# Scoring half of a cross attention inside the query projection, and starting the output projection head by head

## The chip, the cores and the metric

The kernel runs on one core of one Trainium2 chip. The metric is the device time of one execution in microseconds (us), the median of several runs. Engines: PE (TensorE, matmuls and transposes, with PEld its weight loads), ACT (ScalarE), DVE (VectorE), POOL (GpSimd), and SP, which here only issues transfers. Each engine runs its own list of instructions in order; they meet at semaphores alone.

## What is computed

A chain of two transformer layers of one kind and one of another, for 256 tokens of width 1024, in float32. Each of the first two layers is: a gated feed-forward (FFN), a mixer (a pooling one in layer 0, a sparse attention, "NSA", in layer 1), a cross attention to 256 memory tokens, and a second FFN. The change touches the cross attention and the NSA mixer.

```python
def memory_cross_attention(h, mem_n, w_q, w_kv, w_o):
    B, S, D = h.shape                      # 1, 256, 1024
    Hx, dh = XATTN_HEADS, XATTN_HEAD_DIM   # 4, 256
    q = (h @ w_q).astype(F32).reshape(B, S, Hx, dh) * dh ** -0.5
    ...
    p = jax.nn.softmax(jnp.einsum('bqhd,bkhd->bhqk', q, k), axis=-1)
    o = jnp.einsum('bhqk,bkhd->bqhd', p, v).reshape(B, S, D)
    return o.astype(h.dtype) @ w_o
```

The NSA mixer projects `h` to queries, keys, values and gates, compresses blocks of keys and values with a small two-layer network, attends to the compressed blocks, to selected blocks and to a window for each of 16 heads, mixes the three by gates, and multiplies by `nsa_w_o`.

## The kernel before

**Weights and products.** A weight matrix is read in slabs of 128x2048 values into four slots of `raw`. ACT copies a slab rounded into `whi` (`split` in ACT's program, line L759), DVE subtracts to get the rest `wlo` (`split` in DVE's, L1308), and PE makes each product of three matmuls (`parts`, L2007 to L2009): high by low, low by high, high by high. A projection to 1024 columns is two chunks of 512; a chunk uses a pair of slots (0 and 1, or 2 and 3) and one half of PSUM's eight banks, the halves taking turns (`half_of_banks`). `chunks` in ACT's and DVE's programs interleaves: the splits for the next chunk (or, in the last chunk, those of the next stage's first chunk, `next_slabs`), and then the evacuation of the present one.

**Cross attention.** The stage `query` makes the queries, transposed, in two chunks; each chunk holds two of the four heads. `cross` then has 8 units, one for each head and half of the tokens. For a unit PE makes the scores (L2211), DVE their maximum (`top`, L1528), ACT the exponentials with their sum (`exps`, L950), DVE the reciprocal and the scaling (`weigh`, L1534 and L1535), PE two transposes (`turn`, L2221), ACT the copy to SBUF (`keep`, L958). For each head PE then makes probabilities times values (`values`, L2230), ACT and DVE split the result into `aT_hi` (L964) and `aT_lo` (L1540). Three buffers are in rotation, and the scores of a unit are made two units ahead. `project` multiplies by `xattn_w_o`.

**Stages.** A stage begins with `enter` (the engine waits until ACT and DVE have both left the stage before) and ends on ACT and DVE with `leave` (a drain, L743 on ACT and L1291 on DVE). `keep_clock(n)` issues n matmuls on zeros (L2048); nothing reads them.

**NSA.** `nsa_compress` has its own four slabs; after it, ahead of the attention's first instructions, ACT and DVE split the first two slabs of `nsa_w_o`. `nsa_attend` has 32 units with a similar chain (L2321 scores, L1644 maximum, L1030 exponentials, L1653 and L1656 scaling, L2332 transposes, L2349 values), and PE issues 20 matmuls on zeros behind its first scores.

## Time and profile before

| | |
|---|---|
| median of 3 runs | 1831.32 us (1831.2 to 1831.63) |
| the profiled execution | 1832.79 us, of which the span of the profile is 1830.7 us |
| granted clock, mean | 0.954 of full |
| PE busy | 1685.5 us (92%) |
| DVE busy | 1037.7 us (57%) |
| ACT busy | 790.0 us (43%) |
| layer 0: second query chunk / cross / projection begins | 307.6 / 320.2 / 347.4 us |
| layer 1: second query chunk / cross / projection begins | 1039.5 / 1052.1 / 1078.2 us |
| layer 1: NSA attention / its projection begins | 921.65 / 997.00 us |

The profiled execution lasted 2.09 us more than its span, and 1.47 us more than the median. In a row of the timeline the numbers are start and duration in us; a bracket at its end holds how long the engine had been idle and what released it. PE's matmuls are pipelined: a row of n instructions lasts longer than n steps by the tail of the last one. The granted clock is 1.00 at 2.4 GHz and 0.50 at 1.2 GHz.

### The profile page before, as it was taken

Reading aid. Unit: us, or ns where it says so; the run is one execution under the profiler, and the core shown is the slowest. Engines: PE = TensorE matmul, PEld = TensorE weight load, DVE = VectorE, ACT = ScalarE, POOL = GpSimd, SP = SyncE. Lnnn points to the kernel's source line nnn. Section 1 sums busy time; section 2 is a strip of 40 time slices with the busy share of each in tenths; the row PEclk is TensorE's granted clock in tenths of the full one; section 3 lists DMA queues with packets and bytes.
Section 4 is the critical chain, followed back from the end, with each engine's and each line's share of the span. In section 5 each row is a group of like instructions: output and inputs, shape, how many; then the busy total and the mean of one; then the engine's idle time right before and its main releaser. Section 6 shows DMA issues by size and latency. Waiting matters only on the chain.

```text
span 1830.7 us, 22314 instructions
## 1 busy us (share of the span) xinstructions
PE 1685.5 (92%) x8595; PEld 1397.0 (76%) x8595; DVE 1037.7 (57%) x1326; ACT 790.0 (43%) x964; POOL 96.7 (5%) x143
## 2 busy tenths in 40 slices
PE   6999987899999999989988989999899877889996
PEld 6788867688888788879865867888688663668885
DVE  4577654467765576655565445554557643655553
ACT  4443432355444344333466336555354433244441
POOL 1000000010100000010000021000100110100000
PEclk8999989999999999999989999999899785899998
DMA  8687625077775487743510416556455220435550
GB/s 289 204 282 262 224 100 188 3 264 262 258 231 188 165 267 269 236 135 96 174 59 30 165 51 204 193 189 203 159 182 202 78 103 5 169 130 203 183 183 23
DMA packets 210195, 311.74 MB, mean 170 GB/s; under 512 B 16537, under 2 KB 145589, under 8 KB 209872
## 3 DMA queue, kind: packets, MB, share of 16 engines
q1 hardware_dynamic: 204112, 288.90, 47.2%
q0 software_dynamic: 6016, 21.94, 3.5%
q8 instruction: 42, 0.69, 0.2%
q14 instruction: 25, 0.20, 0.0%
HBM read 306.59 MB, written 4.21 MB: 170 GB/s over the span
## 4 chain that ended last, share of the span: by engine, by line
PE 84%; DVE 6%; ACT 3%; issue 3%; DMA 1%; PEld 1%; POOL 1%; DVEq 0%; PEldq 0%; ACTq 0%; SPq 0%; POOLq 0%
PE ps L2007 25%; PE ps L2009 24%; PE ps L2008 24%; DVE wlo L1308 1%; PE ps L2129 1%; PE ps L2048 1%; PE ps L2230 1%; DMA area<-in_gate_b 1%; PE ps L2058 1%; PE ps L2211 1%; PE ps L2349 1%; ACT xn L1030 1%; PE ps L2436 1%; ACT xn L813 0%; DMA raw<-in_xattn_w_kv 0%
## 5 line engine op out<-in xcount | busy, mean ns | idle before, releaser
L1308 DVE TENSOR_TENSOR wlo<-raw,whi 128x2048 fp32r<-128x2048 f32 x255 | 582.0, 2302 | 237.3 <-ACT whi L759 236.4
L759 ACT ACTIVATE whi<-raw 128x2048 fp32r<-128x2048 f32 x255 | 481.2, 1910 | 206.2 <-PE ps L2009 182.7
L2007 PE MATMUL ps<-wlo,aT_hi 128*128 128x512 f32 (+1 forms) x1280 | 499.3, 390 | 22.8 <-DVE aT_lo L1334 9.2
L2009 PE MATMUL ps<-whi,aT_hi 128*128 128x512 f32 (+1 forms) x1280 | 492.6, 385 | 0.0
L2008 PE MATMUL ps<-whi,aT_lo 128*128 128x512 f32 (+1 forms) x1280 | 492.5, 385 | 0.0
L2007 PEld LDWEIGHTS ps<-wlo,aT_hi 128*128 128x128 f32 x1280 | 243.3, 190 | 73.0 <-issue 14.6
L2009 PEld LDWEIGHTS ps<-whi,aT_hi 128*128 128x128 f32 x1280 | 242.9, 190 | 47.8
L2008 PEld LDWEIGHTS ps<-whi,aT_lo 128*128 128x128 f32 x1280 | 243.5, 190 | 44.9
L2007 PE MATMUL ps<-wlo,hT_hi 128*128 128x512 f32 x480 | 188.0, 392 | 5.4 <-DVE hT_lo L1425 3.0
L2009 PE MATMUL ps<-whi,hT_hi 128*128 128x512 f32 x480 | 187.6, 391 | 0.0
L2008 PE MATMUL ps<-whi,hT_lo 128*128 128x512 f32 x480 | 187.3, 390 | 0.0
L2007 PE MATMUL ps<-aT_lo,whi 128*128 128x256 f32 x600 | 173.4, 289 | 14.8 <-DVE wlo L1308 9.1
L2008 PE MATMUL ps<-aT_hi,wlo 128*128 128x256 f32 x600 | 172.7, 288 | 0.0
L2009 PE MATMUL ps<-aT_hi,whi 128*128 128x256 f32 x600 | 172.5, 288 | 0.0
L2007 PEld LDWEIGHTS ps<-aT_lo,whi 128*128 128x128 f32 x600 | 117.9, 196 | 16.5 <-issue 11.9
L2008 PEld LDWEIGHTS ps<-aT_hi,wlo 128*128 128x128 f32 x600 | 117.9, 197 | 0.1
L2009 PEld LDWEIGHTS ps<-aT_hi,whi 128*128 128x128 f32 x600 | 118.0, 197 | 0.0
L2007 PEld LDWEIGHTS ps<-wlo,hT_hi 128*128 128x128 f32 x480 | 90.4, 188 | 25.3 <-issue 4.1
L2009 PEld LDWEIGHTS ps<-whi,hT_hi 128*128 128x128 f32 x480 | 90.5, 189 | 18.9
L2008 PEld LDWEIGHTS ps<-whi,hT_lo 128*128 128x128 f32 x480 | 90.5, 189 | 18.8
L872 ACT ACTIVATE hT_hi<-ps 128x512 fp32r<-128x512 f32 x44 | 26.3, 598 | 154.8 <-PE ps L2129 154.8
L1350 DVE SCALAR_TENSOR_TENSOR gain<-raw,area,gain 128x256 f32<-128x256 f32 x168 | 81.4, 484 | 5.1
(301 smaller groups left out, 1329.1 us busy)
## 6 DMA issues: line engine op xcount, KB each, us to landing
raw<-in_ffn_w_in SPq DMA_DIRECT2D x176, 512.0 KB, 4.9
raw<-in_ffn_w_out SPq DMA_DIRECT2D x88, 512.0 KB, 4.4
raw<-in_w_ff SPq DMA_DIRECT2D x64, 512.0 KB, 4.8
raw<-in_ada_w SPq DMA_DIRECT2D x48, 512.0 KB, 5.6
raw<-in_w_in SPq DMA_DIRECT2D x48, 512.0 KB, 4.6
raw<-in_xattn_w_kv SPq DMA_DIRECT2D x32, 512.0 KB, 6.9
raw<-in_xattn_w_q SPq DMA_DIRECT2D x16, 512.0 KB, 5.1
raw<-in_xattn_w_o SPq DMA_DIRECT2D x16, 512.0 KB, 4.9
```

The lines of the kernel that those rows point to most:

```text
L759: act.activation(to, of, ACT.Copy).then_inc(hi_ready[slot], 1)
L872: act.activation(hT_hi[:, 0:2, :], ps[:, 6, :], ACT.Copy).then_inc(hT_hi_made, 1)
L1030: last = act.activation(Pb[u % 4][:, c:c + n], Pb[u % 4][:, c:c + n], ACT.Exp, scale=-1.0, bias=nmx4[:, b + j:b + j + 1], accum_out=den4[: ...
L1308: dve.tensor_tensor(lo, of, hi, ALU.subtract).then_inc(lo_ready[slot], 1)
L1350: ins = dve.scalar_tensor_tensor(out=acc, in0=w, scalar=condT[:, k:k + 1], in1=acc, op0=ALU.mult, op1=ALU.add)
L2007: pe.matmul(o, lh, rl, start=start, stop=False, skip_group_check=True)
L2008: pe.matmul(o, ll, rh, start=False, stop=False, skip_group_check=True)
L2009: return pe.matmul(o, lh, rh, start=False, stop=stop, skip_group_check=True)
L2048: pe.matmul(ps[:, bank, :], zero[:, 0:P], zero[:, :], start=True, stop=True, skip_group_check=True)
L2058: last = pe.transpose(ps[:, banks[b], P * k:P * k + P], xn[:, t, P * f:P * f + P], ident)
L2129: last = pe.transpose(ps[:, 6, S * k + P * t:S * k + P * t + P], hs[:, t, HI + P * k:HI + P * k + P], ident)
L2211: last = pe.matmul(ps[:, u % 3, 0:S], qT[:, 2 * h + j, t * P:(t + 1) * P], kT[:, 2 * h + j, :], start=j == 0, stop=j == 1)
```

## The change

The four parts:

- **Scores inside the second query chunk.** After the first of the chunk's four outputs PE makes the scores of units 0 to 3 (heads 0 and 1, whose queries the first chunk gave). DVE takes their maxima between its two splits, ACT the exponentials between its two, and DVE scales all four behind its second split, ahead of evacuating the chunk.
- **A new order of the cross attention.** Four buffers instead of three; PE: transposes of units 0 to 3, scores of 4 to 7, values of heads 0 and 1, transposes of 4 to 7, values of heads 2 and 3. The 12 matmuls on zeros are gone. The outputs' low halves are made last on DVE.
- **Projections wait per head.** PE no longer waits for the stage to end ahead of `project` (cross and NSA): it waits for `o_kept` of a head where it first reads it.
- **NSA.** The two splits of `nsa_w_o`'s first chunk move into `nsa_compress`, and 8 matmuls on zeros are left of 20.

```diff
-            def chunks(count, evac, doubled=(), transfers=(), after=None):
+            def chunks(count, evac, doubled=(), transfers=(), after=None, within=None):
                 for c in range(count):
-                    if c + 1 == count:
+                    if c + 1 == count and within:
+                        split(2 * (count % 2))
+                        within[1]()
+                        split(2 * (count % 2) + 1)
+                    elif c + 1 == count:
                         next_slabs(2 * (count % 2))
...
+                    chunks(2, evac, within=(None, lambda: [self.cross_exps(u) for u in range(4)]))
...
-                    exps(0)
-                    exps(1)
-                    for u in range(8):
+                    for u in range(4):
                         keep(u)
-                        if u + 2 < 8:
-                            exps(u + 2)
-                        if u % 2 == 0 and u:
-                            out_hi(u // 2 - 1)
+                    for u in range(4, 8):
+                        self.cross_exps(u)
+                    out_hi(0)
+                    out_hi(1)
+                    for u in range(4, 8):
+                        keep(u)
+                    out_hi(2)
                     out_hi(3)
...
+                        if v == 0:
+                            split(0)
                         done.next(2 * v)
                         act.wait_ge(consumed[2 * v + 1], done.next(2 * v + 1))
                         act.activation(hid_rows[v], ps[0:4 * N_CMP, v, 0:CMP_HID],
                                        ACT.Gelu_apprx_tanh).then_inc(gelu_made, 1)
+                        if v == 0:
+                            split(1)
...
                     leave()
-                    next_slabs()
...
+                    chunks(2, evac, within=(lambda: [self.cross_top(u) for u in range(4)],
+                                            lambda: [self.cross_weigh(u) for u in range(4)]))
...
+                    if between and j == 1:
+                        between()
                     for k in range(KD):
                         s, r = k // 4, k % 4
+                        if ready and ready(j, k):
+                            pe.wait_ge(o_kept, ready(j, k))
...
+                    def scores():
+                        pe.wait_ge(act_evac, chunk_no.n - 1)
+                        pe.wait_ge(dve_evac, chunk_no.n - 1)
+                        for u in range(4):
+                            self.cross_score(u)
+
+                    chunk(2, 512, turned(bank()), between=scores)
...
-                    score(0)
-                    score(1)
-                    keep_clock(12, 5)
-                    for u in range(8):
-                        if u + 2 < 8:
-                            score(u + 2)
+                    for u in range(4):
                         turn(u)
-                        if u % 2 == 0 and u:
-                            values(u // 2 - 1)
+                    pe.wait_ge(act_evac, chunk_no.n)
+                    pe.wait_ge(dve_evac, chunk_no.n)
+                    for u in range(4, 8):
+                        self.cross_score(u)
+                    values(0)
+                    values(1)
+                    for u in range(4, 8):
+                        turn(u)
+                    values(2)
                     values(3)
                     units.next(8)
                     groups.next(4)
+                    self.heads_ready = lambda j, k: groups.n - 3 + k // 2 if k % 2 == 0 else 0
...
-                    keep_clock(20, 4)
+                    keep_clock(8, 4)
...
+                    self.heads_ready = lambda j, k: groups.n - 1 + j if k == 0 else 0
```

**PE, the end of layer 0's query projection and the cross attention.** Before; ahead of the first row stand the second chunk's 96 matmuls, behind the last one those of the projection:

```order
L2211 MATMUL ps<-area 128x256 x4
L2048 MATMUL ps<-zero 128x512 x12
L2211 MATMUL ps<-area 128x256 x2
L2221 MATMUL ps<-cst,xn 128x128 x2
L2211 MATMUL ps<-area 128x256 x2
L2221 MATMUL ps<-cst,xn 128x128 x2
L2211 MATMUL ps<-area 128x256 x2
L2221 MATMUL ps<-cst,xn 128x128 x2
L2230 MATMUL ps<-area 128x256 x4
```

Of the change; L2239 are scores, L2253 transposes, L2262 values, and between the first row and the second stand the 72 matmuls of the chunk's last three outputs:

```order
L2239 MATMUL ps<-area 128x256 x8
...
L2253 MATMUL ps<-cst,xn 128x128 x8
L2239 MATMUL ps<-area 128x256 x8
L2262 MATMUL ps<-area 128x256 x8
L2253 MATMUL ps<-cst,xn 128x128 x8
L2262 MATMUL ps<-area 128x256 x8
```

The scores of four units have moved into the chunk, the zeros are gone, and what was interleaved unit by unit stands in blocks of four.

**DVE at the same place.** Before (L1516 evacuates a query chunk):

```order
L1516 TENSOR_SCALAR area<-ps 128x512 [waits consumed1]
L1308 TENSOR_TENSOR wlo<-raw,whi 128x2048 [waits hi_ready0]
L1308 TENSOR_TENSOR wlo<-raw,whi 128x2048 [waits hi_ready1]
L1516 TENSOR_SCALAR area<-ps 128x512 [waits consumed3]
L1528 TENSOR_REDUCE small<-ps 128x1 [waits scored,stage_act,stage_dve]
L1528 TENSOR_REDUCE small<-ps 128x1 [waits scored]
```

Of the change (L1538 evacuates, L1548 is the maximum, L1323 the split; behind the last row but one stand three more pairs L1554, L1555):

```order
L1538 TENSOR_SCALAR area<-ps 128x512 [waits consumed1]
L1323 TENSOR_TENSOR wlo<-raw,whi 128x2048 [waits hi_ready0]
L1548 TENSOR_REDUCE small<-ps 128x1 [waits scored] x4
L1323 TENSOR_TENSOR wlo<-raw,whi 128x2048 [waits hi_ready1]
L1554 RECIPROCAL small<-small 128x1 [waits exped]
L1555 TENSOR_SCALAR xn<-xn,small 128x256 [waits dve_step]
...
L1538 TENSOR_SCALAR area<-ps 128x512 [waits consumed3]
```

Four maxima and four scalings now stand ahead of the evacuation of the second chunk, and the second split waits for ACT's, which stands behind four exponentials.

**ACT in NSA's compression.** Before (L1013 is the Gelu, L1055 the attention's first instruction), and then of the change (L761, L1027, L1070):

```order
L759 ACTIVATE whi<-raw 128x2048 x2
L1013 ACT_TABLE_LOAD
L1013 ACTIVATE xn<-ps 60x256 x2
L1016 ACTIVATE gain<-ps 128x60
L1018 ACTIVATE gain<-ps 15x256
L759 ACTIVATE whi<-raw 128x2048 x2
L1055 ACT_TABLE_LOAD
```

```order
L761 ACTIVATE whi<-raw 128x2048 x3
L1027 ACT_TABLE_LOAD
L1027 ACTIVATE xn<-ps 60x256
L761 ACTIVATE whi<-raw 128x2048
L1027 ACTIVATE xn<-ps 60x256
L1032 ACTIVATE gain<-ps 128x60
L1034 ACTIVATE gain<-ps 15x256
L1070 ACT_TABLE_LOAD
```

The two splits ahead of the attention stand before and behind the first Gelu.

## Rows read from the trace of the kernel before

**Rows 1.** The page's first part: busy time and instructions of each engine.

```profile
PE 1685.5 (92%) x8595; PEld 1397.0 (76%) x8595; DVE 1037.7 (57%) x1326; ACT 790.0 (43%) x964; POOL 96.7 (5%) x143
```

**Rows 2.** Groups by line, PE, 1051.5 to 1078 us (layer 1's cross).

```profile
L2211 PE MATMUL ps<-area 128*128 128x256 f32 x32 | 8.1, 382 | 0.9 <-DVEq L1291 0.9
L2230 PE MATMUL ps<-area 128*128 128x256 f32 x32 | 7.7, 383 | 0.5 <-ACT area L958 0.5
L2221 PE MATMUL ps<-cst,xn 128*128 128x128 f32 x16 | 3.3, 290 | 4.2 <-DVE xn L1535 4.2
L2048 PE MATMUL ps<-zero 128*128 128x512 f32 x12 | 3.1, 406 | 0.0
```

**Rows 3.** Timeline of PE, layer 0 (first row) and layer 1.

```profile
307.62 0.28 PE L2007 MATMUL ps<-aT_lo,whi 128*128 128x256 f32 x1
...
1039.53 0.28 PE L2007 MATMUL ps<-aT_lo,whi 128*128 128x256 f32 x1
...
1052.13 1.75 PE L2211 MATMUL ps<-area 128*128 128x256 f32 x7 [0.92 <-DVEq L1291]
...
1064.08 1.03 PE L2211 MATMUL ps<-area 128*128 128x256 f32 x4
...
1078.17 0.47 PE L2007 MATMUL ps<-wlo,aT_hi 128*128 128x512 f32 x1 [1.50 <-ACTq L743]
```

**Rows 4.** Timeline of ACT, layer 0 (first row) and layer 1.

```profile
321.98 1.28 ACT L950 ACT_TABLE_LOAD   x1 [2.05 <-DVE small L1528]
...
1040.22 3.71 ACT L759 ACTIVATE whi<-raw 128x2048 fp32r<-128x2048 f32 x2
...
1053.91 0.47 ACT L950 ACTIVATE xn<-ps,small 128x256 f32<-128x256 f32 x1 [2.07 <-DVE small L1528]
...
1057.96 0.38 ACT L958 ACTIVATE area<-ps 128x256 f32<-128x256 f32 x1 [2.80 <-PE ps L2221]
```

**Rows 5.** Timeline of DVE, layer 1's cross.

```profile
1053.37 0.42 DVE L1528 TENSOR_REDUCE small<-ps 128x1 f32<-128x256 f32 x1 [1.43 <-PE ps L2211]
...
1054.51 0.16 DVE L1534 RECIPROCAL small<-small 128x1 f32<-128x1 f32 x1
1054.71 0.35 DVE L1535 TENSOR_SCALAR xn<-xn,small 128x256 f32<-128x256 f32 x1
```

**Rows 6.** Stretches: length, busy time by engine, granted clock, DMA share, GB/s.

```profile
343.70:351.00 7.30, 5.79 (x16) 4.15 (x15) 2.35 (x2) 4.29 (x3) 0.00 (x0) 0.55 0.01 2
927.60:930.90 3.30, 3.30 (x10) 2.61 (x9) 3.20 (x13) 1.65 (x8) 0.00 (x0) 0.55 1.01 382
937.40:944.10 6.70, 5.64 (x26) 3.95 (x28) 5.67 (x30) 4.37 (x15) 0.00 (x0) 0.50 0.01 4
```

**Rows 7.** Timeline of DVE at the first chunk's end of the output projections.

```profile
359.94 1.28 DVE L1576 TENSOR_TENSOR x<-x,ps 128x512 f32<-128x512 f32 x2 [6.10 <-PE ps L2009]
...
1089.35 1.28 DVE L1576 TENSOR_TENSOR x<-x,ps 128x512 f32<-128x512 f32 x2 [4.71 <-PE ps L2009]
1091.45 7.60 DVE L1308 TENSOR_TENSOR wlo<-raw,whi 128x2048 fp32r<-128x2048 f32 x2 [0.81 <-ACT whi L759]
...
1100.23 1.29 DVE L1576 TENSOR_TENSOR x<-x,ps 128x512 f32<-128x512 f32 x2 [1.19 <-PE ps L2009]
```

**Rows 8.** Timeline of POOL, layer 1's output projection.

```profile
1087.63 9.26 POOL L640 TENSOR_TENSOR area<-area 1x1024 f32<-1x1024 f32 x3 [6.61 <-DMA area<-in_ada_b]
```

**Rows 9.** Timeline of PE and DVE at the start of NSA's attention.

```profile
926.31 6.42 PE L2048 MATMUL ps<-zero 128*128 128x512 f32 x20
...
933.73 0.66 PE L2332 MATMUL ps<-cst,xn 128*128 128x128 f32 x4
...
923.67 4.49 DVE L1308 TENSOR_TENSOR wlo<-raw,whi 128x2048 fp32r<-128x2048 f32 x2 [3.77 <-ACT whi L759]
...
934.31 0.42 DVE L1644 CUSTOM_DVE_ANT_0 xn<-ps,cst 128x256 f32<-128x256 f32 x1 [0.89 <-PE ps L2332]
```

**Rows 10.** Timeline of PE where NSA's output projection begins.

```profile
997.00 0.47 PE L2007 MATMUL ps<-wlo,aT_hi 128*128 128x512 f32 x1 [1.04 <-ACTq L743]
```

More of the change, by code:

```diff
@@ L175, in build @@
         nmx4, den4, rec4 = small[:, 26:34], small[:, 34:42], small[:, 42:50]
+        cross_P = [xnf[:, 256 * b:256 * b + 256] for b in range(4)]
+        cross_bank = (2, 3, 6, 7)
         spare = gain[:, 1, :]
@@ L1308, in split, with chunks @@
                 dve.tensor_tensor(lo, of, hi, ALU.subtract).then_inc(lo_ready[slot], 1)
-            def chunks(count, evac, doubled=(), after=None):
+            def chunks(count, evac, doubled=(), after=None, within=None):
                 for c in range(count):
-                    if c + 1 == count:
+                    if c + 1 == count and within:
+                        split(2 * (count % 2))
+                        within[0]()
+                        split(2 * (count % 2) + 1)
+                        within[1]()
+                    elif c + 1 == count:
                         next_slabs(2 * (count % 2))
@@ L1520, in cross @@
                 def cross(self, l):
                     enter()
[L1523 to L1536 removed]
+                    of_values = half_of_banks(chunk_no.n - 1)
@@ L1545, in cross @@
[L1545 to L1551 removed]
+                    for u in range(4, 8):
+                        self.cross_top(u)
+                    for u in range(4, 8):
+                        self.cross_weigh(u)
+                    for h in range(4):
+                        out_lo(h)
@@ L1620, in nsa_compress @@
                                           ALU.subtract).then_inc(aT_made, 1)
-                    split(2)
-                    split(3)
+                    for s in (2, 3, 0, 1):
+                        split(s)
                     for v in range(2):
@@ L2009, in parts, with chunk @@
                 return pe.matmul(o, lh, rh, start=False, stop=stop, skip_group_check=True)
-            def chunk(pair, n, outs):
+            def chunk(pair, n, outs, ready=None, between=None):
                 before = chunk_no.next() - 2
@@ L2199, in query, with cross_score @@
                     enter()
-                    for c in range(2):
-                        chunk(2 * c, 512, turned(bank()))
-                def cross(self, l):
-                    enter()
-                    def score(u):
-                        h, t = u // 2, u % 2
-                        if u >= 3:
-                            pe.wait_ge(exped, units.n + u - 2)
-                        for j in range(2):
-                            last = pe.matmul(ps[:, u % 3, 0:S], qT[:, 2 * h + j, t * P:(t + 1) * P], kT[:, 2 * h + j, :],
-                                             start=j == 0, stop=j == 1)
-                        last.then_inc(scored, 1)
+                    chunk(0, 512, turned(bank()))
+                    def scores():
[4 more added lines that the diff above has]
+                    chunk(2, 512, turned(bank()), between=scores)
+                def cross_score(self, u):
+                    h, t = u // 2, u % 2
+                    if u >= 4:
+                        pe.wait_ge(exped, units.n + u - 3)
+                    for j in range(2):
+                        last = pe.matmul(ps[:, cross_bank[u % 4], 0:S], qT[:, 2 * h + j, t * P:(t + 1) * P], kT[:, 2 * h + j, :],
+                                         start=j == 0, stop=j == 1)
+                    last.then_inc(scored, 1)
+                def cross(self, l):
+                    stages.next()
+                    of_values = half_of_banks(chunk_no.n - 1)
                     def turn(u):
@@ L2220, in turn @@
                         for m in range(2):
-                            last = pe.transpose(ps[:, 3 + u % 2, P * m:P * m + P], Pb[u % 3][:, P * m:P * m + P], ident)
+                            last = pe.transpose(ps[:, 4 - of_values + u % 2, P * m:P * m + P], cross_P[u % 4][:, P * m:P * m + P], ident)
                         last.then_inc(probs_turned, 1)
@@ L2229, in values @@
                             for m in range(2):
-                                last = pe.matmul(ps[:, 6 + h % 2, S * j:S * j + S],
+                                last = pe.matmul(ps[:, of_values + h % 2, S * j:S * j + S],
                                                  vm[:, m, 256 * h + P * j:256 * h + P * j + P], PTc(h)[:, m, :],
@@ L2246, in cross @@
                     groups.next(4)
+                    self.heads_ready = lambda j, k: groups.n - 3 + k // 2 if k % 2 == 0 else 0
                 def project(self, w, gated=False, part=None):
-                    enter()
                     if gated:
+                        enter()
                         turn_rows()
                         pe.wait_ge(aT_made, c_turned.next(4))
+                    else:
+                        stages.next()
                     for c in range(2):
-                        chunk(2 * c, 512, rows(bank()))
+                        chunk(2 * c, 512, rows(bank()), ready=None if gated or c else self.heads_ready)
                     if part == 0:
```

63 lines of the change are left out of this document (26 added, 37 removed).

## The prediction

> **What bounds the kernel now.** I first read the page: PE is busy 92% of the span, DVE 57%, ACT 43% [rows 1]. So time is to be had where PE waits, or works at the low clock, or does work that nobody reads. Next I read the groups by line for layer 1's cross attention [rows 2] with the timeline of its ends [rows 3]. The second query chunk starts at 1039.53 (the 97th matmul of the stage; the chunk's 96 matmuls end, tail included, at 1052.13 - 0.92 = 1051.21, so without the tail of 0.16 they take 11.5 us), and the projection's first matmul stands at 1078.17: 38.64 us from one to the other. PE's necessary work in them, counted start to start: a score is 4 instructions of 0.217 (four last 1.03, less the tail of 0.38, over three [rows 3]), 0.86 us, and there are 8; values are 8 instructions, 1.73 us, four times; a unit's two transposes about 0.25, eight times; the 12 on zeros 12 x 0.215 = 2.6. So 11.5 + 6.9 + 6.9 + 2.0 + 2.6 = 29.9, and 38.6 - 29.9 = 8.7 us are waits (the idle column shows 0.9 + 0.5 + 4.2 [rows 2] and 1.5 ahead of the projection [rows 3]; the rest is the tail of what ran before each wait). Most of it is for DVE's scaling: PE makes two scores and then wants a transpose whose probabilities still go through maximum, exponential and scaling.
>
> Layer 0 has the same shape, but its chunk starts at 307.62 and the first x-update of the projection stands at 359.94 [rows 3, 7], 52.3 us, against 1089.35 - 1039.53 = 49.8 in layer 1. The stretches say why: from 343.7 to 351.0 the granted clock averages 0.55 with PE busy 5.79 of 7.30 us [rows 6]. In NSA the chain of work starts late, since DVE's two splits run until 928.2 before the first maximum [rows 9], and its projection waits 1.04 us for ACT's drain [rows 10].
>
> **The change, part by part.** Times from the start of the second query chunk, layer 1; a hand-over between engines costs about 0.05 us (maximum 53.37 + 0.42, exponential 53.91, less 0.12 [rows 4, 5]), a drain some 0.2.
>
> *Inside the chunk.* PE: first output 0 to 2.9, four scores to 6.3, three outputs to 15.0 (11.5 + 4 x 0.86). ACT: evacuation, then its first split 0.7 to 2.6 (3.71 for two [rows 4]). DVE: its first split 2.7 to 4.9 (4.49 for two [rows 9]), then the maxima at 4.9, 5.2, 5.7 and 6.5 (0.34 apart, later ones wait for the score). ACT: exponentials of 0.46 each at 5.4, 5.8, 6.3 and 7.0, second split to 9.4. DVE: second split to 11.7, four scalings at 0.45 (reciprocal 0.19, scaling 0.26 to the next start [rows 5]) to 13.5. PE's chunk ends at 15.0, so the evacuation isn't held up: 1.5 us to spare. In layer 0 a table load of 1.28 us stands before the first exponential [rows 4] and leaves 0.2. So three units' worth of waits are paid under 8.6 us of matmuls.
>
> *After the chunk.* Transposes 0 and 1 run at once. The third needs the first copy by ACT, which stands behind evacuation and both drains: copies from 16.05, third transpose at 16.5, a wait of 1.0. Scores 4 to 7 and values of heads 0 and 1 run from 17.0 to 23.9 without a wait, while DVE and ACT do the second four units. The seventh transpose waits 0.6, since the copies of units 4 and 5 (0.28 each; 0.38 long [rows 4]) stand on ACT behind the second output's copy. Values of heads 2 and 3 end at 29.05. The projection reads head 0 first and heads 2 and 3 after 2.7 and 4.1 us, when their low halves have been made (about 28.9 and 30.7). So 27.3 us of work + 1.7 of waits = 29.0. Layer 1 gains 38.6 - 29.0 = **9.6**: 2.6 of zeros and 7.0 of waits. Layer 0: 52.3 - (29.0 + 1089.35 - 1078.17 = 11.2) = **12.1**, if the low stretch goes. I take that, because the waits left to PE come to 1.7 us where they were 8.7, and layer 1 kept its clock with the old ones.
>
> *Given back in layer 1.* POOL starts its loads and three additions for the modulation when DVE leaves the cross. That was 0.05 us after PE began the projection and is now about 1.7 us after (two passes over 128x512 for the last output's halves, and a drain). The additions last 9.26 us [rows 8], and DVE's two splits beside them took 7.60 us where two take 4.49 elsewhere [rows 7, 9]. If they take turns, DVE has 4.5 us of its own and 1.7 us more of POOL's ahead of it: it ends at 1099.05 + 1.7, 20.9 + 1.7 = 22.6 us after the projection's start instead of 20.9, and the x-update which begins at 22.05 [rows 7] is held by 0.6 to 0.85 with the start. I take **-0.8**. Bounds: 0 (they share) and 1.7. The Trainium skill, page "SBUF — State Buffer", says that a VectorE instruction with two SBUF inputs and GpSimd's reads lock each other out for a whole instruction. By that rule the sum has the 0.8; with shared bandwidth it would have 0. The 7.60 against 4.49 agrees with the rule.
>
> *NSA's start.* In `nsa_compress` the two splits stand where ACT and DVE wait for PE, so I cost them at nothing there; the cover is PE's second set of compression matmuls (48 of 0.12 us, 5.8), and without it the pair costs 4.5 on DVE. In the attention, DVE's first maximum comes when its splits end, 923.67 + 4.49 = 928.2 [rows 9]; without them it can come with the first scores, at about 922.3. But PE's 64 small matmuls for compressed scores end 0.6 us (a pair of scores) ahead of the zeros at 926.31, whatever happens, and DVE then goes on with those, 3 us earlier than now. PE drops 12 of 20 on zeros: they last 6.42 [rows 9], with the clock at 0.55 for half of it [rows 6]. The first 8 take about 2.2 (six at 0.215, two at 0.43), scores behind them 2.1 at low clock, so the first transpose comes at 930.6 instead of 933.73 and DVE's next maximum, which waits for it (934.31 [rows 9]), 3.2 earlier. That is **-3.2**; bounds 0 (the chain regains its old pace from something later) and 4.4 (full clock: the scaling, at 929.3, is then the limit).
>
> *NSA's projection.* PE starts when its last values are done, not 1.04 later [rows 10]: **-1.0**.
>
> *Nothing:* slot 1's next slab (FFN) is asked for some 6 us later in either cross; the projection's 22 us lie ahead of its use. The waits per head add ten checks to PE's list, each of which is already met.
>
> **Sum.** -12.1 - 9.6 + 0.8 - 3.2 - 1.0 = -25.1. The profiled execution lasted 1832.79, so it would be 1807.7; the median shown is 1.47 below the profiled one, which gives 1831.3 - 25.1 = **1806.2 us**.
>
> **Rivals.**
> - *The second chunk's evacuation comes late (0.15).* DVE now holds it behind two splits, four maxima, four scalings. For: layer 0 has 0.2 us to spare. Against: layer 1 has 1.5. Price: each us of delay beyond that holds everything behind; with 1 to 4 us in both layers, 1808 to 1814. The Trainium skill, page "ScalarE: Activation LUTs", section on what a table load costs, gives 1.28 us and another 1.38 for a drain at each switch. By that layer 0 would lose 1.2 of its 12.1. The trace shows 1.28 alone: the exponential follows at once.
> - *The clock takes NSA's gain (0.12).* Twelve matmuls on zeros fewer, and the clock is low from 937.4 to 944.1 already [rows 6], with 5.64 us of PE work. If a further such stretch falls into the attention, half of its busy time, about 2.8 us, is lost, or with two, 5.6: 1809 to 1812.
> - *Better (0.12).* The start shifts by the full 4.4 and one or two low stretches in or behind NSA (each 3.4 of PE's time at half) don't occur: 1799 to 1803.
> - *Slower (0.04).* The clock falls in the cross itself, with the zeros gone there, and stays low. PE has 27.3 + 22 us of work per layer from the chunk to the projection's end; at half clock that costs 49 us in a layer. It decides once 25 us are lost, which takes half of one layer's stretch at half clock, or a quarter of both; one layer low throughout gives 1855. Against it: PE works 27.3 of 29.0 us up to the projection, where it was 29.9 of 38.6.
> - *No change (0.03).* The FFN behind each projection is held by its transfers and not by PE, so that an earlier start ends in a wait. Then 1831. Against it: the 12.1, 9.6 and 4.2 would all have to vanish, and PE is the chain nearly throughout.
>
> **How the numbers follow.** The forecast as added up, with the small terms at either bound, gives 1803 to 1809 and has 0.50; late evacuation 0.15, the clock in NSA 0.12, better 0.12, slower 0.04, none 0.03, and 0.04 for several of the small losses together (1814 to 1827). A range of 1799 to 1815 leaves out some 0.12 and with the edges of the cases about 0.2. A difference of 0.2% (3.7 us) is about what a measurement of this kernel can tell from no change: faster 0.93, within it 0.03, slower 0.04.
>
> **What would show it.** In the changed profile: from the start of the second query chunk to the projection some 29 us in both layers, with four scores 2.9 us after the chunk's start and no low clock there; DVE's evacuation of that chunk within 0.3 us of PE's last matmul; two idle times of PE of about 1.0 and 0.6 in the cross; in layer 1 the splits beside POOL's additions ending after PE's last projection matmul; NSA's first transpose about 9 us after the attention's start, where it was 12.1. The prediction is wrong if a new wait of PE for DVE's evacuation appears behind the chunk, or if the stretches behind the projections grow by what those ahead shrink.

## The result and the profile after

The changed kernel takes 1803.04 us (median of 4 runs, 1800.09 to 1803.9), the kernel before, on the same chip, 1831.26 us (4 runs, 1830.82 to 1831.63): the ratio is 0.9843, with a 95% interval of 0.9826 to 0.986. It is 28.2 us faster; 25.1 were forecast. The profiled execution lasted 1800.09 us (span 1798.2); it is the shortest of the four, so that the two profiles lie 32.5 us apart where the medians lie 28.2.

The page's first part: PE is busy 20.0 us less than before [rows 1] in a span that is 32.5 us shorter.

```profile
span 1798.2 us, 22229 instructions
PE 1665.5 (93%) x8559; PEld 1384.3 (77%) x8559; DVE 1038.5 (58%) x1326; ACT 789.9 (44%) x964; POOL 96.6 (5%) x143
```

The groups by line of layer 1's chunk end and cross attention, PE (busy, mean ns of one | idle ahead of them and what ended it), which answer to [rows 2]:

```profile
L2239 PE MATMUL ps<-area 128*128 128x256 f32 x32 | 7.2, 379 | 0.0
L2262 PE MATMUL ps<-area 128*128 128x256 f32 x32 | 7.2, 379 | 0.0
L2253 PE MATMUL ps<-cst,xn 128*128 128x128 f32 x16 | 2.6, 279 | 1.5 <-ACT area L969 1.5
```

The 4.2 us ahead of the transposes, for DVE's scaling, are gone; 1.5 us for ACT's copies are left. PE's timeline from layer 0's second query chunk to the projection, which answers to [rows 3]:

```profile
306.05 0.28 PE L2026 MATMUL ps<-aT_lo,whi 128*128 128x256 f32 x1
...
308.93 0.59 PE L2239 MATMUL ps<-area 128*128 128x256 f32 x2
...
321.02 0.60 PE L2253 MATMUL ps<-cst,xn 128*128 128x128 f32 x4
322.53 0.69 PE L2253 MATMUL ps<-cst,xn 128*128 128x128 f32 x4 [0.92 <-ACT area L969]
323.06 3.62 PE L2239 MATMUL ps<-area 128*128 128x256 f32 x16
326.51 3.62 PE L2262 MATMUL ps<-area 128*128 128x256 f32 x16
329.96 0.60 PE L2253 MATMUL ps<-cst,xn 128*128 128x128 f32 x4
331.18 0.69 PE L2253 MATMUL ps<-cst,xn 128*128 128x128 f32 x4 [0.62 <-ACT area L969]
331.70 3.62 PE L2262 MATMUL ps<-area 128*128 128x256 f32 x16
334.97 0.58 PE L2026 MATMUL ps<-wlo,aT_hi 128*128 128x512 f32 x1
```

From 306.05 to 334.97 are 28.92 us, with the first score 2.88 after the start and two waits of 0.92 and 0.62. Layer 1 has the same from 1021.29 on. DVE at the same place (idle time in the bracket), for [rows 5]:

```profile
308.68 2.29 DVE L1323 TENSOR_TENSOR wlo<-raw,whi 128x2048 fp32r<-128x2048 f32 x1 [1.74 <-ACT whi L761]
310.89 1.25 DVE L1548 TENSOR_REDUCE small<-ps 128x1 f32<-128x256 f32 x3
...
315.44 2.29 DVE L1323 TENSOR_TENSOR wlo<-raw,whi 128x2048 fp32r<-128x2048 f32 x1 [2.44 <-ACT whi L761]
...
321.22 0.69 DVE L1538 TENSOR_SCALAR area<-ps 128x512 f32<-128x512 f32 x1 [1.64 <-PE ps L2028]
```

DVE stands idle for 1.64 us ahead of the evacuation (its copy of the chunk's result out of PSUM) until PE is done, so the four maxima and four scalings put ahead of it hold nothing up.

**By stretch.** The time up to the start of DVE's last x-updates (an x-update adds a result to `x`) was cut at seven of its instructions: the evacuation of each first query chunk, the first x-update of each output projection (cross attentions and NSA), an evacuation of NSA's first projection, and the x-update at layer 1's end. In parentheses stands an estimate of the PE time lost to the low clock (a granted clock of 0.50): (1 - granted clock) x busy time, summed over stretches of 1 us. It is too high where PE would have waited for another engine anyway, as in NSA. "Cross" runs from the first query chunk's evacuation to the projection's first x-update.

| us | before | before, second profile | after | after, second profile |
|---|---|---|---|---|
| start to second query chunk | 307.82 (7.8) | 306.52 (5.4) | 306.25 (6.0) | 305.83 (5.4) |
| cross, layer 0 | 52.12 (2.7) | 51.16 (1.6) | 40.02 (0) | 40.02 (0) |
| to NSA | 478.78 (1.7) | 477.07 (0) | 477.08 (0) | 477.30 (0) |
| NSA | 169.47 (7.9) | 171.37 (9.4) | 166.60 (8.5) | 166.53 (8.3) |
| to layer 1's query chunk | 31.54 (0) | 31.54 (0) | 31.54 (0) | 31.55 (0) |
| cross, layer 1 | 49.62 (0) | 51.08 (1.5) | 40.04 (0) | 40.04 (0) |
| second FFN | 205.93 (0) | 205.92 (0) | 205.96 (0) | 205.92 (0) |
| third layer to the end | 522.52 (42.1) | 521.32 (40.1) | 517.79 (36.6) | 520.89 (40.4) |

In the first pair of profiles the cross attentions gave 12.10 and 9.58 us, NSA 2.87; 8.0 us come from stretches that the change doesn't touch, where 9.0 us less were lost to the clock. In the second pair the cross attentions gave 11.14 and 11.04.

### The profile page after: what moved, and what is told of

It reads as the page before. It is cut to its first block, busy times and chain, and to the rows that moved or that the text cites. A ratio compares the mean times of both kernels' runs of the same rounds, so it can differ in the third digit from the quotient of the medians.

```text
span 1798.2 us, 22229 instructions
## 1 busy us (share of the span) xinstructions
PE 1665.5 (93%) x8559; PEld 1384.3 (77%) x8559; DVE 1038.5 (58%) x1326; ACT 789.9 (44%) x964; POOL 96.6 (5%) x143
## 4 chain that ended last, share of the span: by engine, by line
PE 85%; DVE 6%; ACT 3%; issue 3%; DMA 1%; PEld 1%; POOL 1%; DVEq 0%; PEldq 0%; ACTq 0%; SPq 0%; POOLq 0%
PE ps L2026 25%; PE ps L2028 25%; PE ps L2027 25%; DVE wlo L1323 1%; PE ps L2152 1%; PE ps L2262 1%; PE ps L2239 1%; DMA area<-in_gate_b 1%; PE ps L2386 1%; PE ps L2081 1%; ACT xn L1045 1%; PE ps L2474 1%; PE ps L2071 1%; ACT xn L819 0%; DMA raw<-in_xattn_w_kv 0%
## 5 line engine op out<-in xcount | busy, mean ns | idle before, releaser
L1323 DVE TENSOR_TENSOR wlo<-raw,whi 128x2048 fp32r<-128x2048 f32 x255 | 583.1, 2305 | 239.7 <-ACT whi L761 238.8
L761 ACT ACTIVATE whi<-raw 128x2048 fp32r<-128x2048 f32 x255 | 481.5, 1910 | 202.8 <-PE ps L2028 179.4
L2026 PEld LDWEIGHTS ps<-aT_lo,whi 128*128 128x128 f32 x600 | 116.3, 194 | 16.2 <-issue 11.6
```

The costliest lines, as they stand in the source:

```text
L761: act.activation(to, of, ACT.Copy).then_inc(hi_ready[slot], 1)
L1323: dve.tensor_tensor(lo, of, hi, ALU.subtract).then_inc(lo_ready[slot], 1)
L2026: pe.matmul(o, lh, rl, start=start, stop=False, skip_group_check=True)
```

## The experiments

In diffs "+" is the experiment's. Each is made from the changed kernel unless it says otherwise. Ratios are to the kernel before, run beside them.

**One part each.** `cross_only` takes NSA's part back (splits, 20 zeros, whole-stage wait there):

```diff
-                    keep_clock(8, 4)
+                    keep_clock(20, 4)
...
-                    self.heads_ready = lambda j, k: groups.n - 1 + j if k == 0 else 0
+                    self.heads_ready = None
```

> The changed kernel with the NSA part undone (splits behind the compression stage, 20 matmuls on zeros, the NSA projection behind the whole stage). Theory: the two cross attentions are worth what their own stretches show in the two traces, 12.1 + 9.6 = 21.7 us, and the 3.6 us of the median beyond all stretches that the change touches (28.2 - 24.6) are the clock in other stages: 1809.6, give or take the clock's steps of 1.7 us. Rival: the NSA part is worth more than the 2.9 us of its stretch, so that this kernel stays at 1812 or above.

Measured: 1807.35 us (1801.66 to 1808.75), before 1832.19; ratio 0.9862 (0.9839 to 0.9884).

`nsa_only` is the kernel before with NSA's part alone:

```diff
-                    keep_clock(20, 4)
+                    keep_clock(8, 4)
...
+                    self.heads_ready = lambda j, k: groups.n - 1 + j if k == 0 else 0
```

> The kernel before with only the NSA part of the change. Theory: its stretch gains 2.9 us, 1828.4. Rival: the low clock moves instead and takes it back (1831), or what was found beyond the touched stretches belongs to it (1824.8).

Measured: 1828.13 us (1823.67 to 1829.99), before 1832.19; ratio 0.9974 (0.9961 to 0.9987). The parts give 24.8 and 4.1 us and so add up to about the whole; the cross is 86% of it. The 24.8 are 3.1 more than the 21.7 of the two cross stretches, which take 40.03 us each in this profile too; of the rest, see the end of the next section.

**The waits per head.** `stage_waits`: PE waits for the whole stage ahead of every projection.

```diff
                 def project(self, w, gated=False, part=None):
+                    enter()
                     if gated:
-                        enter()
                         turn_rows()
...
-                        chunk(2 * c, 512, rows(bank()), ready=None if gated or c else self.heads_ready)
+                        chunk(2 * c, 512, rows(bank()))
```

> The changed kernel, but PE waits for the end of the stage ahead of all output projections, as before. Theory: after PE's last values come ACT's high half (0.6 us), DVE's low half (0.7), a drain and the hand-overs, 1.75 us in each cross attention and 1.0 in NSA: +4.5, so 1807.5. Rival: the wait is covered since DVE's and ACT's next splits are the limit anyway: 1803.

Measured: 1810.12 us (1808.0 to 1812.48); ratio 0.9879 (0.9858 to 0.9899). Both cross stretches take 41.75 and 41.74 us instead of 40.02 and 40.04. PE's timeline of this kernel at layer 1's projection has the wait back:

```profile
1059.55 0.47 PE L2026 MATMUL ps<-wlo,aT_hi 128*128 128x512 f32 x1 [1.50 <-ACTq L745]
```

The waits per head are worth 1.7 us in each cross. The median is some 7 us above the changed kernel's instead of 4.5; the profile shows where more went: NSA's stretch takes 171.10 us with 12.2 lost to the clock, against 166.60 with 8.5.

**The scores inside the chunk.** `scores_behind`: the first four scores, maxima, exponentials and scalings stand behind the second query chunk; both splits ahead of them.

```diff
-                    chunk(2, 512, turned(bank()), between=scores)
+                    chunk(2, 512, turned(bank()))
+                    scores()
...
-                    chunks(2, evac, within=(None, lambda: [self.cross_exps(u) for u in range(4)]))
+                    chunks(2, evac)
+                    for u in range(4):
+                        self.cross_exps(u)
```

> The changed kernel, but the first four scores, maxima, exponentials and scalings come behind the second query chunk, and both splits ahead of them. The new order in blocks of four stays. Theory of the prediction's text (waits of three units are paid under the chunk's matmuls): most of the 7 us of waits per layer come back, up to +14, 1817. Rival: the blocks of four do nearly all of it; worked through from the rows, PE waits 1.2 us for the first scaling, 0.2 for the second and 0.2 more for the first copy, 1.5 us per layer: +3.0, 1806.

Measured: 1810.9 us (1806.22 to 1812.57); ratio 0.9877 (0.9855 to 0.9898). Layer 1's cross stretch takes 41.58 us, only 1.54 more than with the scores inside (layer 0's 43.26 has 1.7 of low clock in it). PE's timeline of this kernel, layer 1: the four scores, then the first, third and seventh transposes.

```profile
1041.96 3.61 PE L2245 MATMUL ps<-area 128*128 128x256 f32 x16
...
1046.55 0.90 PE L2259 MATMUL ps<-cst,xn 128*128 128x128 f32 x4 [0.98 <-DVE xn L1560]
1048.48 0.69 PE L2259 MATMUL ps<-cst,xn 128*128 128x128 f32 x4 [1.03 <-ACT area L971]
...
1057.13 0.69 PE L2259 MATMUL ps<-cst,xn 128*128 128x128 f32 x4 [0.62 <-ACT area L971]
```

Four scores in a row cover the chain of unit 0 (maximum, exponential, scaling) but for 0.98 us, even behind the chunk. So most waits are gone without the place inside the chunk.

**The changed kernel once more.** `after_again`:

> The changed kernel once more. Theory: all stretches without touched code and without low clock have the same length to 0.1 us, and what differs between two profiles of one kernel is the number of stretches at the low clock, each costing up to 1.7 us of PE's time per step; median 1803 to 1806. Rival: the stages behind the touched ones are faster because of the change, then their lengths repeat too.

Measured: 1803.16 us (1801.49 to 1805.9), before 1829.81; ratio 0.9855 (0.9841 to 0.9869). Its stretches are in the table. Only the last differs from the first profile by more than 0.5 us, namely by 3.1. The windows view of a piece of it, first profile and then second (length, busy time by engine, granted clock, DMA share, GB/s):

```profile
1400.00:1530.00 130.00, 101.06 (x472) 72.05 (x471) 59.83 (x163) 50.33 (x124) 14.08 (x13) 0.74 0.23 77
```

```profile
1400.00:1530.00 130.00, 101.37 (x456) 71.19 (x454) 58.37 (x162) 50.45 (x124) 11.86 (x12) 0.71 0.19 68
```

The same program, at 0.74 and 0.71 of the clock, is 16 matmuls less far at the same time.

**DVE's slack in the chunk.** `dve_late` puts 4.98 us of further DVE work between the scalings and the evacuation of the second chunk, in both layers (four maxima over 128x1024, read by nobody):

```diff
+                    def late():
+                        for u in range(4):
+                            self.cross_weigh(u)
+                        for _ in range(4):
+                            step(dve.tensor_reduce(small[:, 63:64], area[:, 0:1024], AX.X, ALU.max))
```

> The changed kernel with four maxima over 128x1024 values (read only, the result is thrown away) on DVE between the four scalings and the evacuation of the second query chunk, some 4.7 us. Theory: DVE has 1.64 us to spare there in both layers (the idle time ahead of the evacuation), and beyond it the whole cross attention moves: (4.7 - 1.6) x 2 = +6, 1809 to 1812. Rival: the third transpose and ACT's copies have room of their own, so that less than half of it is seen (+3 or less).

Measured: 1815.71 us (1812.86 to 1819.32), before 1829.81; ratio 0.9924 (0.9912 to 0.9937). DVE's timeline, layer 0:

```profile
321.58 4.98 DVE L1545 TENSOR_REDUCE small<-area 128x1 f32<-128x1024 f32 x4
326.59 0.69 DVE L1538 TENSOR_SCALAR area<-ps 128x512 f32<-128x512 f32 x1
```

The evacuation's idle time of 1.64 is gone, and PE waits 4.18 us ahead of the third transpose instead of 0.92. Layer 1's cross grew from 40.04 to 44.99, of which 1.7 is low clock: 3.3 us, which is 4.98 - 1.64. The rest of the 12.6 us in the medians is low clock (3.0 in layer 0's cross, where there was none) and what the stretches around it vary by.

**The zeros.** `before_no_zeros` is the kernel before without its 12 matmuls on zeros in the cross attention:

```diff
                     score(1)
-                    keep_clock(12, 5)
                     for u in range(8):
```

> The kernel before without the 12 matmuls on zeros in each cross attention. Theory: the first transpose was held by them from 1055.1 to 1057.5, so each cross is 2.4 us shorter: -4.8, if the clock holds. Rival: they kept the clock up; then a stretch of 3.4 us or more at the low level falls into the cross or the projection behind it, and the gain is 1 us or nothing.

Measured: 1826.03 us (1818.73 to 1829.49), before 1829.81; ratio 0.9976 (0.9963 to 0.9988). The cross stretches take 48.55 and 47.27 us, both at full clock. In layer 1 that is 2.35 less than 49.62; in layer 0 it is only some 1.0 less than what either profile of before shows once its low clock is taken off (52.12 less 2.7, 51.16 less 1.6). PE's timeline, layer 0 (first row) and layer 1, has the reason: in layer 0 the first transposes wait 1.43 us for DVE's scaling, in layer 1 0.16.

```profile
322.40 0.44 PE L2221 MATMUL ps<-cst,xn 128*128 128x128 f32 x2 [1.43 <-DVE xn L1535]
...
1049.04 2.83 PE L2211 MATMUL ps<-area 128*128 128x256 f32 x12 [0.92 <-DVEq L1291]
1052.03 0.44 PE L2221 MATMUL ps<-cst,xn 128*128 128x128 f32 x2 [0.16 <-DVE xn L1535]
```

The 1.27 between them is ACT's table load (1.28 us), which stands ahead of layer 0's first exponential [rows 4]; beside the zeros it cost nothing. In this profile the zeros aren't needed for the clock: without them it didn't fall in either cross, and with them it fell in five of the six other cross stretches that have the old order (1.5 to 2.7 us each). The median is 3.8 us lower, of which these two stretches explain some 3.4.

`nsa_20_zeros` is the changed kernel with NSA's 20 zeros:

```diff
-                    keep_clock(8, 4)
+                    keep_clock(20, 4)
```

> The changed kernel with 20 matmuls on zeros again ahead of NSA's attention. Theory: DVE's maximum of unit 4 waits for the first transpose, which they hold up; 12 of them at 0.215 (some at 0.43) are 2.6 to 3.4 us, less nothing: the first transpose at 11.5 us behind the compressed scores as before, and nearly all of the 2.75 us is lost, +2.7. Rival: the splits that moved bring the gain and the zeros only fill a wait: no change.

Measured: 1810.58 us (1807.83 to 1812.85), before 1829.81; ratio 0.9896 (0.9881 to 0.9911). That is 7.4 us above `after_again` instead of the 2.7 expected; in the profile NSA's stretch takes 170.64 us (9.3 lost to the clock), 4.1 more than there, and 1.5 are in the low clock of the stretch behind it (33.03 instead of 31.55).

`splits_behind` keeps the 8 zeros and puts the two NSA splits back behind the compression:

```diff
                     for v in range(2):
-                        if v == 0:
-                            split(0)
                         done.next(2 * v)
...
                     leave()
+                    next_slabs()
```

> The changed kernel with the two splits behind the compression stage again, but 8 matmuls on zeros. Theory: DVE's first maximum is back at the end of its splits, and the first scaling is then done 10.1 us behind the start of the compressed scores; the first transpose stands there, between 8.8 (changed) and 11.5 (before): 1.3 of the 3.3 us (taken without the clock) are lost. Rival 1: the zeros alone were the brake, nothing is lost. Rival 2: the splits are the brake, all is lost.

Measured: 1807.6 us (1803.83 to 1808.07), before 1831.05; ratio 0.9869 (0.9846 to 0.9892). PE's timeline at NSA's start of these three kernels, in the order changed, 20 zeros, splits behind:

```profile
906.28 0.71 PE L2358 MATMUL ps<-area 64*128 64x128 f32 x8 [0.48 <-ACTq L745]
...
910.94 3.20 PE L2071 MATMUL ps<-zero 128*128 128x512 f32 x8
914.07 1.60 PE L2358 MATMUL ps<-area 64*128 64x256 f32 x8
915.61 0.66 PE L2369 MATMUL ps<-cst,xn 128*128 128x128 f32 x4
```

```profile
912.48 6.46 PE L2071 MATMUL ps<-zero 128*128 128x512 f32 x20
...
919.94 0.66 PE L2369 MATMUL ps<-cst,xn 128*128 128x128 f32 x4
```

```profile
911.35 3.18 PE L2069 MATMUL ps<-zero 128*128 128x512 f32 x8
...
917.38 0.44 PE L2367 MATMUL ps<-cst,xn 128*128 128x128 f32 x2 [1.29 <-DVE xn L1673]
```

Counted from the start of the 64 small matmuls, the first transpose comes at 8.8 us in the changed kernel, at 11.6 with 20 zeros (before: 11.5) and at 10.1 with the splits behind, there with a wait for DVE's scaling. So the zeros hold the start; the splits decide only once the zeros are few: then they are worth 1.4 us at the first transpose. In the whole of NSA that gain can't be told from the clock: with the splits behind, the stretch takes 167.44 us (9.5 lost) against 166.60 (8.5). The start moves with the clock as well: in `stage_waits` and `scores_behind`, which have the changed kernel's NSA start, the first transpose comes at 10.4 us, with the clock low from about 2 us on.

**The kernel before once more**, for a second profile of it. `before_again`:

> The kernel before once more, for its profile. Theory: low-clock stretches fall by chance; without them its cross attentions are 49.6 us from the second query chunk to the projection's first update (49.6 in layer 1 before, 52.1 with a low stretch in layer 0), its NSA stretch about 161.5, and all behind the second layer's feed-forward about 480.4 once PE's time lost to the low clock is taken off. Rival: the part behind, 522.5 us in the three profiles with the old cross attention and 517.0 to 520.9 in the seven with the new one, is longer for a reason of its own and shows 522 again without more low clock.

Measured: 1833.92 us (12 runs, 1828.05 to 1836.76) against 1831.05 for its 17 partners; ratio 1.0005 (0.999 to 1.0021). The table has its stretches.

**One step on.** `finer` takes scores and transposes in smaller blocks, so that ACT's copies aren't waited for, and makes NSA's second pair of scores ahead of the 64 small matmuls, with no zeros:

```diff
-                    for u in range(4):
-                        turn(u)
+                    turn(0)
+                    turn(1)
...
+                    self.cross_score(4)
+                    turn(2)
+                    turn(3)
...
                     values(0)
+                    turn(4)
+                    turn(5)
                     values(1)
...
                     score_pair(0)
+                    score_pair(1)
...
-                    score_pair(1)
-                    keep_clock(8, 4)
```

> A further version of the changed kernel. Cross: PE makes the scores of unit 4 ahead of the transposes of units 2 and 3, and the transposes of units 4 and 5 ahead of the values of head 1, with ACT's copies in the same order; the two waits of 0.92 and 0.62 us go, 1.1 us less per layer by hand. NSA: PE's second pair of scores ahead of the 64 small matmuls, no matmuls on zeros, DVE's work on the compressed scores behind the scaling of unit 1: the first transpose 5.9 us behind the attention's start instead of 9.3, but DVE's compressed part then follows, so 2.3 us less. In all -4.5 without the clock: 1798 to 1800. Rival: without zeros the clock falls in NSA (each low stretch of 3.4 us costs up to 1.7), and the NSA part gives nothing: 1801 or more.

Measured: 1800.52 us (1795.91 to 1801.97), before 1831.05; ratio 0.9827 (0.9806 to 0.9849): the lowest of all, though its interval overlaps those of the changed kernel. It is 2.5 to 2.6 us below that kernel's two medians instead of the 4.5 expected. The groups by line of its cross, PE, layer 1:

```profile
L2257 PE MATMUL ps<-cst,xn 128*128 128x128 f32 x16 | 2.4, 272 | 0.0
L2243 PE MATMUL ps<-area 128*128 128x256 f32 x32 | 7.5, 381 | 0.4 <-ACT area L946 0.4
```

Both cross stretches take 38.6 us (40.0), which is the 1.54 of waits less 0.4 that are left, and some tails; NSA takes 160.70 (5.1) instead of 166.60 (8.5), of which 3.4 is clock and 2.5 a shorter chain, so that the rival (the clock takes it back) isn't borne out there; the second FFN takes 1.1 more, and 1.7 and 1.5 were lost to the clock ahead of and behind NSA.

## Why the prediction was right, and where its reasons were not

**The cross attentions: the sum right, the credit in it misleading.** 12.1 and 9.6 us were forecast, 12.10 and 9.58 measured; 29.0 us from chunk to projection, 28.92 measured; waits of 1.0 and 0.6, measured 0.92 and 0.62. The schedule of the changed kernel was worked out right, row by row. But the sentence that gives a reason, "three units' worth of waits are paid under 8.6 us of matmuls", credits the place of the scores, and that place is worth 1.54 us of the 7.0. (The zeros themselves took 2.93 us in layer 1 and not 2.6, as they follow each other by 0.23 and not 0.215; without them PE has 0.16 more to wait.) Layer 1's 9.58 is made up of 2.35 for the zeros, 1.70 for the waits per head and 1.54 for the place of the scores; the remaining 4.0 is a difference, not an experiment of its own, and falls to the order in blocks of four with four buffers, taken together. (`scores_behind` has that order and the waits per head, `before_no_zeros` neither: 41.58 and 47.27, which is 5.7 = 1.7 + 4.0.) It is close to the 4.2 us that PE waited for scalings before [rows 2]. The new order and the new place came in one step, and nothing in the sum tells them apart.

**Layer 0's 2.5 us for the low clock** were counted as a sure gain. The second profile of before has a low stretch in both cross attentions (1.6 and 1.5). Of the eight cross stretches with the old order profiled here (before twice, `nsa_only`, `before_no_zeros`), five lost 1.5 to 2.7 us to it; of 14 with the new one (changed twice, `cross_only`, `stage_waits`, `nsa_20_zeros`, `splits_behind`, `finer`) none did. It came back only where DVE or ACT was made late (`dve_late` in both layers, `scores_behind` in one). So the gain is real, but can lie with either layer: that 12.1 and 9.6 came out layer by layer is luck, since the second pair of profiles has 11.14 and 11.04, with nearly the same sum.

**The table load** was to leave 0.2 us of slack in layer 0. It left 1.64, as in layer 1. ACT's timeline:

```profile
306.75 1.90 ACT L761 ACTIVATE whi<-raw 128x2048 fp32r<-128x2048 f32 x1
308.67 1.28 ACT L957 ACT_TABLE_LOAD   x1
...
311.34 0.47 ACT L957 ACTIVATE xn<-ps,small 128x256 f32<-128x256 f32 x1 [1.39 <-DVE small L1548]
```

Here ACT loads the table straight behind the split, before the exponential's wait for the maximum, and then stands idle for 1.39: the load is hidden. In the kernel before the same load stood behind the wait, 0.10 us after the maximum (321.46 + 0.42) and ahead of the exponential by its whole length [rows 4]; there the wait for the end of the stage stands ahead of it as well. The prediction took the load's place over from that row. A late evacuation, the main rival, was 1.64 us away in both layers; `dve_late` shows that the mechanism is there from that point on. The Trainium skill, page "ScalarE: Activation LUTs", section "What ACT_TABLE_LOAD costs", puts a drain of 1.38 us beside a load. The rows above can't tell, as the idle 1.39 could hide it; but in `scores_behind` the load stands at 320.20, 0.02 us behind the activation before it, and the exponential follows 0.01 us behind its end, so there is none, and the measurement decides.

**The 0.8 us to be given back to POOL's additions** didn't come. POOL and DVE in layer 1's projection:

```profile
1060.73 9.27 POOL L642 TENSOR_TENSOR area<-area 1x1024 f32<-1x1024 f32 x3 [5.81 <-DMA area<-in_ada_b]
```

```profile
1061.53 1.28 DVE L1596 TENSOR_TENSOR x<-x,ps 128x512 f32<-128x512 f32 x2 [2.98 <-PE ps L2028]
1063.62 8.52 DVE L1323 TENSOR_TENSOR wlo<-raw,whi 128x2048 fp32r<-128x2048 f32 x2 [0.81 <-ACT whi L761]
1072.41 0.69 DVE L1596 TENSOR_TENSOR x<-x,ps 128x512 f32<-128x512 f32 x1 [0.26 <-PE ps L2028]
```

POOL's additions start 10.52 us after the projection's first matmul (9.46 before [rows 3, 8]): 1.06 later, not 1.7, as POOL is through with issuing its loads 1.86 later but then waits 5.81 us for them instead of 6.61. The pair of splits slows from 7.60 to 8.52, ends 2.14 us after the additions as it did before (2.16), and DVE still has 0.26 idle ahead of the x-update (1.19 before), which stands 10.88 us behind the chunk's first in both kernels. Price 0, the lower bound. So the mechanism, taking turns, is right, and the size of the shift was off: 1.06 fits into DVE's slack of 1.19. One by one the instructions show the turns. The second addition (1063.20, 2.40 us) runs as long as the first; the split that starts at 1063.62 ends at 1067.75, 2.15 after that addition; the third addition, from 1065.67, takes 4.32 us, and ends 2.24 after the split; the second split ends 2.15 after the third addition. The Trainium skill, page "SBUF — State Buffer", section "Who interferes with whom", has a VectorE instruction with two SBUF inputs and a GpSimd instruction that reads SBUF block each other; the trace agrees with these times.

**NSA's start: -3.2 forecast, -2.75 measured** (first transpose 9.33 us after the attention's start, 12.08 before [rows 9]). The mechanism is right and the size was off by the 8 zeros, which took 3.13 us and not 2.2, as the clock was at half from 911.8 on (windows below); the scores behind them took 1.54 instead of 2.1. At the projection the lead is 3.9 us (70.9 against 74.8, from the start of the 64 small matmuls; 71.0 against 74.9 in the second profiles). **The hand-over's -1.0** is in that and is shown: PE goes from the last values into the projection without a wait. PE's timeline there, changed kernel and `before_again`, and the windows of the changed kernel:

```profile
974.11 3.68 PE L2386 MATMUL ps<-area 128*64 128x256 f32 x16
977.72 0.80 PE L2026 MATMUL ps<-wlo,aT_hi 128*128 128x512 f32 x1
```

```profile
988.30 3.68 PE L2349 MATMUL ps<-area 128*64 128x256 f32 x16
993.02 0.77 PE L2007 MATMUL ps<-wlo,aT_hi 128*128 128x512 f32 x1 [1.03 <-ACTq L743]
```

```profile
911.80:912.60 0.80, 0.80 (x3) 0.66 (x2) 0.77 (x2) 0.00 (x0) 0.00 (x0) 0.50 0.00 0
...
966.00:973.00 7.00, 3.93 (x28) 2.29 (x28) 2.77 (x9) 4.50 (x13) 0.00 (x0) 1.00 0.01 2
973.50:980.30 6.80, 6.80 (x27) 3.81 (x24) 0.42 (x1) 1.92 (x2) 0.00 (x0) 0.53 0.00 0
```

The last values run at half clock in both, and so does the projection's start (its first matmul takes 0.80 and 0.77), while the one profile that the forecast was made from has it at full clock [rows 10]. So that pair of profiles shows 2.87 us for NSA's stretch and the second pair 4.84, on either side of the 4.2 forecast. PE had been busy 3.93 of the 7 us ahead of the low stretch, and 1.00 of the clock was granted in them.

**The other 3 us.** The sum with the terms as measured in the first pair of profiles (12.1, 9.6, 0 and 2.9) is 24.6; the medians moved by 28.2, and in `after_again`'s comparison by 26.7. The forecast has no term for the rest. It lies in stretches that the change leaves alone, and in the profiles nearly all of it is clock: the last stretch took 521.3 to 522.5 us in four profiles with the old cross attention, 517.0 to 520.9 in nine with the new, and without the time lost to the clock 480.1 to 482.7 in all of them. Run by run the clock goes with the time too: the three groups of 17 executions of the kernel before have correlations of -0.87, -0.55 and -0.88 between mean granted clock and time, and in the first, with clocks of 0.951 to 0.960 and times of 1836.6 to 1826.7, it is about 1 us for each 0.001. All nine profiles with the new cross attention lie below all four with the old; were the thirteen in a random order, that would happen once in 715 times, so luck isn't the likely explanation. A third layer that starts some 5 us earlier isn't enough either: `nsa_only` and `before_no_zeros` have it and keep 522.2 and 522.1. The kernels with the new cross attention start it 14 to 33 us earlier. What spares it low stretches stays open: no run was made that shifts that layer by as much without another change.

**The rival that said slower** (clock low throughout the cross, without its zeros) isn't borne out by `before_no_zeros`, nor by any of the 14 new cross stretches. **No change** is refuted too: the FFN behind the projection kept its 205.9 us and began earlier.

## What to carry to other kernels

Where one engine waits for a chain through others unit by unit, first make its independent work in larger blocks with as many buffers: here that was worth some 4 us in a cross attention (by difference), and lifting the block into the stage before only 1.5 more. Where an engine issues matmuls on zeros ahead of useful work that is nearly ready, try the kernel without them and look at the granted clock both times: here 12 of them cost 2.35 us in one layer and some 1.0 in the other, and the clock didn't need them. When a change is judged by a sum that comes out right, undo its parts one by one all the same; and when the profile of a kernel has low-clock stretches, take a second profile of before, since a single one showed 2.5 us of low clock in layer 0 as though it belonged to that layer.

## What was not expected of the hardware

- The low clock's stretches fall differently in executions of one kernel: 36.6 and 40.4 us were lost in the same 520 us of the same program, and 17 executions of the kernel before spread over 9.8 us.
- A table load can be done ahead of the wait of the activation that needs it (308.67, with the activation's input ready at 311.3), or behind the waits, as in the kernel before (321.98, with the input ready at 321.9). On the chain it cost 1.27 us (`before_no_zeros`, layer 0 against layer 1).
- The clock fell while NSA's matmuls on zeros ran (from 0.90 in 911.0 to 911.8 to 0.50 behind it): eight took 3.20 us and 20 took 6.46, where 0.23 each, as in layer 1's cross attention before at full clock, would be 1.8 and 4.6.
- The pair of DVE splits beside POOL's 1x1024 additions takes 7.60 to 8.52 us instead of 4.49: each waits for the addition under way to end, and the third addition, which takes 2.4 us undisturbed, takes 4.32 beside a split. The pair ended 2.1 us after POOL in both kernels.
